# Filler pieces behind every second level set, two at a time, in two decay mixers of a transformer block

## The reference

```python
b = jnp.cumsum(gc, axis=2)
diff = b[:, :, :, None, :] - b[:, :, None, :, :]
decay = jnp.where(causal, jnp.exp(jnp.where(causal, diff, 0.0)), 0.0)
scores = jnp.einsum('bhtd,bhsd,bhtsd->bhts', qc, kc, decay)
o = jnp.einsum('bhts,bhse->bhte', scores, vc) + jnp.einsum('bhtd,bhde->bhte', qc * jnp.exp(b), S)
```

## Time and profile before

| what | value |
|---|---|
| median of 3 runs | 3463.9 us (3462.42 to 3464.08) |
| span of the profiled execution, first to last instruction | 3462.0 us |
| what lies around the span, by the median | 1.9 us |
| mean granted PE clock | 0.996 |
| busy: PE, DVE, ACT, POOL | 98%, 47%, 37%, 46% of the span |
| stretch of the hgrn mixer | about 530 to 730 us |
| stretch of the gla mixer | about 735 to 925 us |

### The profile page before, as it was taken

The page is one execution under the profiler, slowest core; times in us unless marked ns, Lnnn a source line. Parts: engine busy times, 40 slices in busy tenths (PEclk is TensorE's granted clock), DMA queues, the critical chain, the costliest instruction groups (busy, mean ns, idle before and its releaser), DMA issues.

```text
span 3462.0 us, 45820 instructions
## 1 busy us (share of the span) xinstructions
PE 3397.3 (98%) x18522; PEld 2742.4 (79%) x18522; DVE 1616.8 (47%) x2172; ACT 1271.8 (37%) x1936; POOL 1577.1 (46%) x1021
## 2 busy tenths in 40 slices
PE   7999999999999999999999999999999999999998
PEld 5888887777777878788888878888886888888886
DVE  7333325545434868655553443033273265444443
ACT  5333325344323555333332355233323352222224
POOL 2322124444422565766664654211122655666666
PEclk9999999999999999999999999999999999999999
DMA  4221123231235523111112333213343331111112
GB/s 119 75 62 56 56 62 96 75 104 43 85 123 179 173 79 107 59 55 55 52 49 82 93 116 120 67 57 96 99 136 101 123 102 43 58 54 54 49 52 88
DMA packets 375889, 290.32 MB, mean 84 GB/s; under 512 B 14561, under 2 KB 342113, under 8 KB 375553
## 3 DMA queue, kind: packets, MB, share of 16 engines
q1 hardware_dynamic: 345216, 241.26, 23.1%
q10 hardware_dynamic: 30464, 46.14, 3.9%
HBM read 238.96 MB, written 48.40 MB: 83 GB/s over the span
## 4 chain that ended last, share of the span: by engine, by line
PE 85%; DVE 4%; POOL 4%; ACT 3%; issue 2%; DMA 1%; SPq 0%; POOLq 0%; ACTq 0%; DVEq 0%
PE psum L1969 26%; PE psum L2587 14%; PE psum L276 14%; PE psum L2617 14%; PE psum L1587 5%; PE psum L1103 2%; PE psum L582 2%; POOL w_lo L1920 1%; PE psum L1634 1%; PE psum L1184 1%; ACT w_hi L1901 1%; POOL m_lo L2083 0%; PE psum L1624 0%; PE psum L1096 0%; PE psum L3235 0%
## 5 line engine op out<-in xcount | busy, mean ns | idle before, releaser
L1920 POOL TENSOR_TENSOR w_lo<-w_raw,w_hi 128x1024 fp32r<-128x1024 f32 (+1 forms) x239 | 573.7, 2400 | 1158.3 <-ACT w_hi L1901 1137.2
L1901 ACT ACTIVATE w_hi<-w_raw 128x1024 fp32r<-128x1024 f32 (+1 forms) x243 | 251.3, 1034 | 461.8 <-PE psum L1969 422.1
L276 PE MATMUL psum<-x_hi,w_hi 128*128 128x512 f32 x832 | 360.2, 433 | 7.2 <-ACT gate L320 3.8
L1969 PE MATMUL psum<-x_hi,w_hi 128*128 128x512 f32 x912 | 341.5, 394 | 2.5 <-DVE w_lo L1929 1.0
L1969 PE MATMUL psum<-x_hi,w_lo 128*128 128x512 f32 x912 | 336.8, 389 | 0.0
L1969 PE MATMUL psum<-x_lo,w_hi 128*128 128x512 f32 x912 | 336.8, 389 | 0.0
L276 PE MATMUL psum<-x_hi,w_lo 128*128 128x512 f32 x832 | 327.5, 394 | 0.0
L276 PE MATMUL psum<-x_lo,w_hi 128*128 128x512 f32 x832 | 326.1, 392 | 0.0
L2625 DVE TENSOR_TENSOR acc<-acc,psum 128x512 f32<-128x512 f32 x336 | 227.0, 685 | 187.5 <-PE psum L2617 187.5
L2487 POOL TENSOR_TENSOR w_lo<-w_raw,w_hi 128x512 fp32r<-128x512 f32 x131 | 183.3, 1399 | 148.2 <-ACT w_hi L2462 148.2
L1969 PEld LDWEIGHTS psum<-x_hi,w_hi 128*128 128x128 f32 x912 | 170.7, 188 | 42.5 <-issue 6.4
(11 more groups left out here) (737 smaller groups left out, 7807.3 us busy)
## 6 DMA issues: line engine op xcount, KB each, us to landing
w_raw<-in_w_in SPq DMA_DIRECT2D x105, 512.0 KB, 4.5
merge_raw<-gates ACTq DMA_DIRECT2D x48, 512.0 KB, 4.5
gates<-gate SPq DMA_DIRECT2D x32, 512.0 KB, 2.9
w_raw<-in_w_ffn_up SPq DMA_DIRECT2D x60, 256.0 KB, 3.0
w_raw<-in_w_ffn_up SPq DMA_DIRECT2D x24, 512.0 KB, 3.8
w_raw<-in_w_mlp_out SPq DMA_DIRECT2D x42, 256.0 KB, 2.7
w_raw<-in_w_mlp_in SPq DMA_DIRECT2D x34, 256.0 KB, 2.9
w_raw<-in_w_ple_gate SPq DMA_DIRECT2D x16, 512.0 KB, 4.2
```

What stands on the lines that cost most here:

```text
L276: last = pe.matmul(bank, w[:, k, :], x[:, k, half(h)], start=(k == 0 and j == 0), stop=(k == KT - 1 and j == 2))
L1901: act.activation(self.view(self.c.wh, i), self.view(self.c.wr, i), ACT.Copy).then_inc(self.sig["w_hi"], 1)
L1920: pool.tensor_tensor(self.view(self.c.wl, i), self.view(self.c.wr, i), self.view(self.c.wh, i).bitcast(F32), ALU.subtract).then_inc(self.s ...
L1969: last = pe.matmul(self.bank(t, h)[0:m, :], w[:, k, col:col + m], x(k)[:, 512 * h:512 * h + 512], start=(k == 0 and n == 0), stop=(k == nk ...
```

## The change

It changes the tables of pieces of two mixers. For hgrn and gla, the sets l1, l3, l5 and l7 get no piece ahead of them, l2, l4 and l6 get two in place of one, and the step kt gets one more. Nothing else is edited; each unit has as many pieces as before.

```diff
@@ hgrn
-                              lambda n: dict(var=1, l0=12 if n == 0 else 5, l1=1, l2=1, l3=1, l4=1, l5=1, l6=1, l7=1, kt=3,
+                              lambda n: dict(var=1, l0=12 if n == 0 else 5, l1=0, l2=2, l3=0, l4=2, l5=0, l6=2, l7=0, kt=4,
                                              psi=2, y=3 if n == 0 else 2),
@@ gla
-                              lambda n: dict(qk=3 if n == 0 else 0, var=1, l0=6 if n == 0 else 5, l1=1, l2=1, l3=1, l4=1,
-                                             l5=1, l6=1, l7=1, kt=2 if n == 0 else 3, psi=2, y=3),
+                              lambda n: dict(qk=3 if n == 0 else 0, var=1, l0=6 if n == 0 else 5, l1=0, l2=2, l3=0, l4=2,
+                                             l5=0, l6=2, l7=0, kt=3 if n == 0 else 4, psi=2, y=3),
```

## The result

| | median, us | lowest to highest, us | profiled execution, us | its span, us |
|---|---|---|---|---|
| before | 3463.9 | 3461.7 to 3465.4 (9 runs) | | 3462.0 |
| after | 3472.8 | 3467.8 to 3476.4 (9 runs) | 3474.6 | 3472.8 |

The nine runs of before hold the three of the table of the kernel before. After to before is 1.0027, 95% interval 1.0017 to 1.0037: the change makes the kernel 8.9 us slower. The runs of after also lie further apart, 8.6 us against 3.7.

The account below looks back on a forecast made before the run. PE was taken as the bound, busy 98% of the span. Span 3462.0 + 2.4 (new waits less saved switching) + 8.0 (clock) = 3472.4, plus 1.9 around the span, 3474.3 us; range 3464 to 3482 us.

Parts of the forecast that it names:

- The seam: PE's way from 128-row filler to 64-row set matmuls and back: 0.42 us, 32 removed, 13.4 us saved.
- The loop: DVE, ACT, POOL chain from one set to the set three later: l3 no earlier than l0 + 8.55 us.
- near 20: PE's waits before L582 for POOL's signal: near 20 us in place of 5.5.
- The account: Waits less saved switching over the eight hgrn and gla units, without the clock: +2.4 us.
- four units together +2.1: Units with w_lo before l3's products, already waiting at l3: +0.52 us net each, +2.1 together.
- five drops from the six gaps: PE's long waits bring five falls to half clock (1.2 GHz), 1.6 us each: +8.0 us.
- the rule of small idles: Small idles between matmul groups lower PE's clock; waits of 1 us would count, some 3 us more.
- Mean clocks about 0.02 lower: Sign in the profile after: PE's mean clocks in the hgrn and gla stretches about 0.02 lower.
- the clock holds: Rival: gaps come, but PE's clock drops twice at most; 3466.3 to 3469.7 us; chance 0.28.
- faster: Rival: l3 and l5 ready by 5.9 us after l0 and l2, all 13.4 us gained, 3450.5 us; chance 0.09.
- priced this at 0.4 us (gla unit 0): Allowance for slower DVE differences in the l2 to l5 loop of gla unit 0: 0.4 us.

Follow-up runs that it names:

- l7 alone: Kernel before with only l6/l7 back to back (l7=0, one piece more ahead of kt) in both mixers: 3462.1 us, ratio 0.9995.
- early doubles alone: Kernel before with only l0/l1 and l2/l3 back to back (l1=0, l2=2, l3=0, l4=2): 3477.6 us, ratio 1.0040.
- w_lo behind the products: Changed kernel with POOL's w_lo split moved from ahead of its level's products to behind them: 3460.7 us, ratio 0.9990 against before.
- the thin w_lo: Changed kernel with w_lo in the level loop computed for 128 of 1024 columns: 3455.1 us; the same cut in the kernel before: 3461.1 us.
- the run with three pieces at l2: Changed kernel with one piece moved from ahead of kt to ahead of l2 (l2=3): 3466.9 us, ratio 1.0009 against before.

## Why the prediction came out as it did

- *The seam, 0.42 us each, 13.4 in all:* right. 0.40 to 0.49 a unit in the run with l7 alone; in the change the second set starts 0.99 us behind the first in place of 2.68. Between the two sets PE nearly keeps the pace that it has between pairs (eight pairs are 0.90), which is what the Trainium skill, "TensorEngine Tiling (Array Packing)", Key Properties, makes of it: no drain without a change of mode. The rule alone would have given the wrong sign.
- *The loop:* right, in place and size. l3 at l0 + 8.52 us for 8.55, PE's wait there 2.42, 2.28, 2.39 and 2.42 in four units and 1.77 in gla unit 3, and 2.65 at l5 in gla unit 0; 20.3 us in all for "near 20", 14.8 of them new. In gla unit 0 luck helped: l5 came 14.30 us behind l0, as forecast, but l2 stood 5.56 behind l0 and not 5.1 (PE waited 0.34 at l1), and the loop from there was 8.74 and not 9.25, so PE waited 2.65 us and not 3.2.
- *The account, +2.4 us:* measured +1.1. Hgrn units 1 and 3 and gla unit 2 are within 0.15 of their terms, gla unit 0 too. For hgrn unit 3 that is in part luck: it was taken for a unit like gla unit 2, without w_lo, but one stands ahead of its l2 (694.18 to 696.55 in after). The term that failed is "four units together +2.1": it took hgrn unit 2 for one like unit 0. In the trace of before, l0 of that unit lay in a stretch at half clock, l3 stood 9.36 us behind it and not 8.55; the change gives back the 0.86 beyond the loop, -0.35 in place of +0.52.
- *The clock, "five drops from the six gaps", +8.0 us:* four gaps brought one, 7.4 us in all, since one of them lasted twice as long (6.82 us, 2.8 us lost). The six gaps, five over 2.2 us and one of 1.77, don't order themselves by length: 1.77 brought a drop, 2.28 and 2.39 none. That where a gap falls can spare it was said; for a single gap the trace of before could not tell it. Over the traces of all twelve kernels, nine of the fourteen waits at a set from 1.76 to 2.65 us brought a drop; the same wait at l3 of gla unit 3 did in after (1.77) and did not with the early doubles alone (1.76). By the rule of small idles that the prediction weighed (the Trainium skill, "TensorE: Matmul & The Clock Gate", psum-queue depth-cycling) the waits of about 1 us would have counted as well. Alone they did not: hgrn unit 3 and gla unit 2 of after have five waits from 0.51 to 0.91 us and no drop, and with w_lo behind the products no drop followed 19 waits up to 1.2 us. Two of them close together did. The drop of before at 603.46 has in front of it these two waits in hgrn unit 1, the second for a gate copy:

```profile
600.63 1.16 PE L582 MATMUL psum<-hgrn_qe,hgrn_ke 64*128 64x128 f32 x16 [0.47 <-POOLq L949]
603.01 0.74 PE L269 MATMUL psum<-hgrn_ident,gate 128*128 128x128 f32 x4 [1.22 <-ACT gate L320]
```

The drops of before at 644.42 and of the kernel with w_lo behind at 643.56 and 803.99 stand behind such pairs too (0.59 and 1.39 us; 0.92 and 1.39). That the small idles count is thus borne out, but not each time: with l7 alone the first pair (0.47 and 1.22 us) brought no drop, nor did in after the pair of 0.59 and 1.39 at 644.73.
- *Total:* the sum for the span was 3472.4, and it is 3472.8, but by misses that cancel: 1.3 less in the account and 0.6 less in the clock, 1.4 more from the opening and 0.9 between and behind the units, neither of which the change touches by its edit. The median, 3472.8 for 3474.3, is 1.8 under the profiled execution, about as much as one drop. Of the other executions only the mean granted clock is recorded: 0.993 in the two longest of after (3476.1 and 3476.4 us), 0.995 in the two shortest (3467.8 and 3469.1). So much of their spread goes with the clock, but the split of the 8.9 us of the medians into waits and clock stays open; only that of the profiled execution is shown.
- *"Mean clocks about 0.02 lower":* wrong for hgrn, 0.99 for 0.98, since two of its old drops went and one came; in gla 0.96 for 0.99, more than forecast.
- *The rivals:* "the clock holds" needed two drops at most; "faster" needed l3 and l5 within 5.9 us, and with the thin w_lo, at 6.62, part of it came in: 6.0 us of the 13.4.

## What to carry to other kernels

Cover for a bound engine may be moved only if the loop that feeds it is shorter than the new distance: here the piece between two sets hid 1.36 us of a DVE, ACT, POOL chain of 8.5 us, and taking 13.4 us of switching away brought 14.8 us of waits. Before such an edit list what stands in each feeding engine's order inside the loop that need not be there (w_lo), move that first, and look at that order again after every edit, since the place of one piece moved it. Where waits can't be removed, short ones that lie apart did less harm here than long ones: no drop followed the 12.6 us in 19 waits, and four followed the 20.3 us with six long ones. No run splits the same total of waits in two ways, and two short ones close together did bring a drop, so this is a hint and no rule.

## What the runs showed of the hardware

- A DVE subtraction (128x256, f32, two inputs) takes 0.42 or 0.43 us when no POOL instruction runs beside it, 0.42 to 1.1 beside one of POOL's products, and 2.57 us when it starts 0.1 us into POOL's w_lo of 2.36 us (562.01 in after), 1.64 where it starts 1.0 us into it, 2.11 at 561.09 in before (0.5 into it), and 0.67 beside the thin one of 0.46. In each of the four beside w_lo it ends 0.28 or 0.29 us behind w_lo. The Trainium skill, "SBUF — State Buffer", SBUF: two separate sides, says that the port pair shared by the two is an exclusive lock for the whole instruction; the rows agree. In all of them POOL was first. The prediction had priced this at 0.4 us (gla unit 0).
- A stretch at half clock lasted twice as long (6.82 us) three times inside a unit: in gla unit 1 of after, and in two units of the run with three pieces at l2. In all three PE was idle again within it (busy 6.18, 6.44 and 6.23 of 6.82). Seven of the twelve traces also have one of 6.83 us between the two mixers, at 738 to 753 us, with PE busy 5.7 to 6.8 of it. Idle time within a stretch does not by itself make it long: the one at 803.99 with w_lo behind had PE busy 3.15 of 3.41 us and stayed single.
- A single gap of PE of 1.77 us cost nearly as much by the clock (1.5 us) as by itself; one of 1.76 us at the same place, with the early doubles alone, cost nothing by the clock.
